# Attention of a two-layer decoder trunk: score products grouped over two PSUM banks, q's inverse RMS applied in the softmax, and a new order of the attention stage on every engine

## The chip, the core and the metric

One core of a Trainium2 chip runs the whole program. The metric is the device time of one execution in microseconds (us). The core has five engines, each with its own instruction stream that it works off in order, and they meet only at semaphores: PE (TensorE, matmuls; its weight loads are listed as PEld), DVE (VectorE), ACT (ScalarE), POOL (GpSimd) and SP (SyncE, which here only issues DMAs). PE writes to PSUM, eight banks of 512 fp32 columns in 128 partitions; DVE and ACT read it.

## The reference

Two layers (DEPTH = 2) over 256 tokens of width 1024. Each layer has a SwiGLU FFN (hidden width 2816), the mixing stage that is changed here, and a second FFN:

```python
x = x + 0.5 * swiglu(rmsnorm(x, ffn1_norm[l]), ...)
h = rmsnorm(x, mix_norm[l])
c_q, c_kv, k_pe, q_s, k_s, v_s = jnp.split(h @ w_in[l], split_idx, axis=-1)
q_a  = (rmsnorm(c_q, ...) @ mla_w_q_b[l])    # 4 heads, 128 plain + 64 rotary columns
kv_a = (rmsnorm(c_kv, ...) @ mla_w_kv_b[l])  # 4 heads, 128 of k + 128 of v
q_a, k_a = rmsnorm(q_a, mla_q_norm[l]), rmsnorm(k_a, mla_k_norm[l])   # per head, then rotary on the 64
out_a = dense_causal_attention(q_a, k_a, v_a, mla_scale)
q_b, k_b = apply_rope(rmsnorm(q_s, ...)), apply_rope(rmsnorm(k_s, ...)) # 8 q heads, 2 k heads, 64 columns
out_b = sliding_window_sink_attention(q_b, k_b, v_b, swa_sinks[l], swa_scale)   # window 128, sinks
x = x + concat(rmsnorm(out_a, ...), rmsnorm(out_b, ...)) @ w_o[l]
x = x + 0.5 * swiglu(rmsnorm(x, ffn2_norm[l]), ...)
```

All products are of fp32 accuracy.

## The kernel before

The order on every engine is written out by hand; there is no scheduler. The 256 tokens are two blocks, t = 0 and t = 1, of 128 rows. The weights come as a stream of halves of 128 x 1024 fp32 through a ring of four raw buffers (SP issues, one DMA for each half). ACT rounds a half to fp32r (`whi`, L444) and DVE subtracts to get the rest (`wlo`, L747); these two are called a split. A large product is three fp32r matmuls, hi x hi, hi x lo, lo x hi (L1125, L1128, L1129; a `product`). The six weight slots are freed by PE as it goes on.

The mixing stage of a layer runs as follows. `input_main` and `input_tail` give the input projection of both blocks in banks A[t] and UV[t]. For each block, ACT and DVE take squares, POOL raises the sums to the power -0.5, DVE normalises (`latent_norm`), PE transposes (`transpose_latent`), and `latent_products` gives the latent heads' q, k and v. Then all of q and k is brought to its final form before it is transposed: `mla_parts` and `mla_sums` (squares of q and k together), one POOL step for both, `mla_norm` and `window_norm` (multiplication by the inverse RMS, the gains, the rotation), `transpose_qk` (17 transposes for each block) and copies to `qt` and `kt`. The scores of a block fill banks A[t][0] and A[t][1] in turn: two latent heads in a bank, then window heads, four in a bank for block 0 and two for block 1. For each head `scores` issues a 128-row fp32 product (L1347), a 64-row one for the rotary part (L1349) and a bf16 product of the identity with the mask (L1351); a window head has a 64-row product (L1355) and a mask (L1357). An fp32 product is listed as two MATMUL instructions (two passes), an fp32r or bf16 one as one. After a bank come `maxima` (DVE), `softmax` (ACT, exponentials with their sums, L644), `transpose_probs` (PE, L1368), `probs_copy` (ACT, L658) and `values` (PE, L1385). Block 0's output is normalised, transposed (`transpose_norm`) and multiplied by `w_o` in eight `output_chunk`s, of which five are put between the banks of block 1; then come block 1's eight, and the second FFN.

Of the kernel before, what the change touches and what calls it, by code (L numbers as in the profile page):

```python
# [17 lines left out]
ALU = mybir.AluOpType  # L18
# [6 lines left out]
P = 128  # L25
D = 1024
# [87 lines left out]
def hybrid_trunk(nc, x_in, stream, norm_gains, norm_cols, small_gains, col_gains, rope, out):  # L114
    with ExitStack() as ctx:
# [23 lines left out]
        rot_in, rot_tmp = rot[:, 0:640], rot[:, 640:1280]  # L139
        attn = sb("attn", [P, D])  # L140
        kpe_g = attn[:, D - ROPE:D]
        kpe = heads(attn[:, 512:512 + TB * ROPE], TB)
        xg = xn
# [9 lines left out]
        probs = work[:, 0:2, :]  # L153
# [12 lines left out]
        consts = sb("consts", [P, 3, 10])  # L166
# [8 lines left out]
        ss_m = sb("ss_m", [P, TB, 8])  # L175
# [28 lines left out]
        rstd_ready = sem("rstd_ready")  # L204
        xn_ready = sem("xn_ready")
# [23 lines left out]
        sum_ready = sem("sum_ready")  # L229
        main_done = sem("main_done")  # L230
# [7 lines left out]
        swa_copied = sem("swa_copied")  # L238
        swa_ss = sem("swa_ss")
        swa_rstd = sem("swa_rstd")  # L240
        swa_used = sem("swa_used")
        mla_done = sem("mla_done")
        mla_squares = sem("mla_squares")
        mla_ss = sem("mla_ss")
        mla_rstd = sem("mla_rstd")
        qkn_ready = sem("qkn_ready")
        qk_psum = sem("qk_psum")
        qk_act = sem("qk_act")
        qk_dve = sem("qk_dve")
# [10 lines left out]
        def norm_no(l, k, t):  # L260

            return (l * NORMS + k) * TB + t

# [53 lines left out]
        def score_banks(t):  # L317
            per = 4 // (t + 1)
            return [(True, [0, 2]), (True, [1, 3])] + [(False, list(range(i, i + per))) for i in range(0, SH, per)]
# [29 lines left out]
        def _(pool):  # L349
# [5 lines left out]
            pool.memset(consts[:, 1, :], EPS)  # L355
            pool.memset(consts[:, 0, :], -0.5)
# [26 lines left out]
            def norm_rstd(l, k, t):  # L383
                n, rs = 2 * norm_no(l, k, t), rs_x[:, t, 0:1]
                if k == 2:
                    pool.wait_ge(ss_ready, n + 2)
                    rstd(rs_x[:, t, :], ss_x[:, t, :], consts[:, 1, 0:2], rstd_ready)
                    return
# [7 lines left out]
                step(pool.tensor_tensor(eps_x[:, t, :], rs.to_broadcast([P, 10]), consts[:, 1, :], ALU.mult))  # L396
# [3 lines left out]
            def latent(l, t):  # L400
                pool.wait_ge(latent_ss, l * TB + (t + 1))
                rstd(rs_c[:, t, :], ss_c[:, t, :], eps_x[:, t, 0:2], latent_rstd)
# [5 lines left out]
            def mla(l, t):  # L408
                pool.wait_ge(mla_ss, l * TB + (t + 1))
                rstd(rs_m[:, t, :], ss_m[:, t, :], consts[:, 1, 0:8], mla_rstd)  # L410

            for l in range(DEPTH):
                norm_rstd(l, 0, 0)
                if l == 0:
                    pool.dma_start(cs[:], rope.rearrange("t p a d -> p t a d")).then_inc(rope_loaded, 16)
                    load_gain(0, 3)
# [4 lines left out]
                load_gain(l, 2)  # L421
# [1113 lines left out]
```

## Time and profile before

| | |
|---|---|
| time, median of 3 runs | 965.27 us (965.18 to 965.64) |
| the profiled execution: its time, its span | 965.41 us, 963.6 us |
| PE busy, PEld busy | 943.1 us, 792.4 us |
| DVE, ACT, POOL busy | 638.8, 527.3, 58.9 us |
| granted TensorE clock | 1.000 of full speed |
| HBM | 171 GB/s over the span |

The span is from the first to the last instruction of the profiled execution. A busy time is the union of the engine's instructions; those of PE overlap at their ends, so what an instruction costs PE is read from one start to the next. The mixing stage of layer 0 lies at about 198 to 300 us, that of layer 1 at about 673 to 776 us.

### The profile page before, as it was taken

To read this page: it belongs to the slowest core of one execution; us is meant where nothing else is said; L and a number is where in the kernel's file an instruction comes from. 1 tells how busy PE (TensorE), PEld (TensorE's weight loads), DVE (VectorE), ACT (ScalarE), POOL (GpSimd) and SP (SyncE) were. 2 spreads that over 40 slices of the span, in tenths; PEclk is the share of its full clock that TensorE was granted. 3 is DMA by queue.
4 is the path that set the end of the run, shared out by engine and by line. 5 is a ranking of instruction groups with operands and counts; after the bars stand their busy time and mean duration, and the time that the engine had idled before them with its cause. 6 is when DMAs were issued, how large, how long until landed. Compare 5 with 4: busy or idle time off the path is not lost. (4 is left out here: it accounts for less than half of the span.)

```text
span 963.6 us, 14627 instructions
## 1 busy us (share of the span) xinstructions
PE 943.1 (98%) x4998; PEld 792.4 (82%) x4998; DVE 638.8 (66%) x941; ACT 527.3 (55%) x1018; POOL 58.9 (6%) x100
## 2 busy tenths in 40 slices
PE   7999999999899999999999999999998999999998
PEld 5888888888677888888878888888876788888887
DVE  5766666677766766666666666667777666666663
ACT  7555555564665655555555555556456655555551
POOL 3000000032111000000010000000330100000000
PEclk9999999999999999999999999999999999999999
DMA  8755555550054765555547555555401547555541
GB/s 303 263 190 186 191 195 184 187 197 2 22 167 151 252 194 192 183 191 195 175 155 236 191 195 183 190 195 175 153 1 49 170 155 235 185 188 196 185 163 44
DMA packets 45812, 165.41 MB, mean 172 GB/s; under 512 B 5296, under 2 KB 5296, under 8 KB 45776
## 3 DMA queue, kind: packets, MB, share of 16 engines
q1 hardware_dynamic: 44496, 160.98, 50.6%
q0 software_dynamic: 992, 3.42, 1.0%
q8 instruction: 23, 0.38, 0.2%
q10 hardware_dynamic: 288, 0.54, 0.1%
q14 instruction: 13, 0.11, 0.0%
HBM read 163.86 MB, written 1.05 MB: 171 GB/s over the span
## 5 line engine op out<-in xcount | busy, mean ns | idle before, releaser
L747 DVE TENSOR_TENSOR wlo<-raw,whi 128x1024 fp32r<-128x1024 f32 x304 | 370.6, 1224 | 130.7 <-ACT whi L444 130.4
L444 ACT ACTIVATE whi<-raw 128x1024 fp32r<-128x1024 f32 x304 | 316.8, 1051 | 10.3 <-DMA raw<-stream 10.3
L1186 PE MATMUL UV<-acts,whi 128*128 128x512 f32 x1280 | 318.9, 391 | 0.0
L1186 PEld LDWEIGHTS UV<-acts,whi 128*128 128x128 f32 x1280 | 234.9, 188 | 46.9 <-DVE wlo L747 1.5
L1193 PEld LDWEIGHTS UV<-acts,wlo 128*128 128x128 f32 x1280 | 174.3, 190 | 12.2
L1193 PE MATMUL UV<-acts,wlo 128*128 128x256 f32 x1280 | 178.8, 282 | 0.0
L1125 PE MATMUL A<-whi,ht_hi 128*128 128x512 f32 x352 | 138.2, 393 | 0.0
L1128 PE MATMUL A<-wlo,ht_hi 128*128 128x512 f32 x352 | 137.9, 392 | 0.0
L1129 PE MATMUL A<-whi,ht_lo 128*128 128x512 f32 x352 | 137.0, 389 | 0.0
L507 ACT ACTIVATE ht_hi<-work 128x256 fp32r<-128x256 f32 x80 | 33.4, 418 | 121.9 <-DVE work L826 121.9
L503 ACT ACTIVATE work<-UV 128x256 f32<-128x256 f32 x80 | 30.7, 383 | 88.7 <-PE UV L1193 88.6
L495 ACT ACTIVATE work<-UV 128x256 f32<-128x256 f32 x80 | 30.6, 383 | 87.0 <-PE UV L1193 87.0
L1129 PEld LDWEIGHTS A<-whi,ht_lo 128*128 128x128 f32 x352 | 66.1, 188 | 14.4
L1125 PEld LDWEIGHTS A<-whi,ht_hi 128*128 128x128 f32 x352 | 66.4, 189 | 11.6
L1128 PEld LDWEIGHTS A<-wlo,ht_hi 128*128 128x128 f32 x352 | 66.4, 189 | 10.7
L821 DVE TENSOR_TENSOR work<-UV,work 128x256 f32<-128x256 f32 x80 | 33.9, 424 | 50.7 <-ACT work L503 50.7
L831 DVE TENSOR_TENSOR ht_lo<-work,ht_hi 128x256 fp32r<-128x256 f32 x80 | 34.0, 425 | 38.7 <-ACT ht_hi L507 38.7
L1125 PE MATMUL A<-whi,acts 128*128 128x512 f32 x136 | 54.9, 403 | 0.0
L1129 PE MATMUL A<-whi,acts 128*128 128x512 f32 x136 | 53.2, 391 | 0.0
L1128 PE MATMUL A<-wlo,acts 128*128 128x512 f32 x136 | 53.0, 390 | 0.0
L817 DVE TENSOR_TENSOR work<-UV,work 128x256 f32<-128x256 f32 x80 | 33.9, 424 | 24.4 <-ACT work L495 24.4
L390 POOL TENSOR_TENSOR sums<-sums,consts 128x1 f32<-128x1 f32 x12 | 9.7, 805 | 585.2 <-ACT qkn L462 369.7
(166 smaller groups left out, 871.2 us busy)
## 6 DMA issues: line engine op xcount, KB each, us to landing
raw<-stream SPq DMA_DIRECT2D x304, 512.0 KB, 3.4
gain<-norm_gains POOLq DMA_DIRECT2D x5, 512.0 KB, 4.8
out<-x SPq DMA_DIRECT2D x4, 256.0 KB, 2.1
sgain<-small_gains POOLq DMA_DIRECT2D x2, 324.0 KB, 4.8
x<-x_in SPq DMA_DIRECT2D x1, 512.0 KB, 3.5
x<-x_in ACTq DMA_DIRECT2D x1, 512.0 KB, 7.6
cs<-rope POOLq DMA_DIRECT2D x1, 128.0 KB, 5.5
cgain<-col_gains POOLq DMA_DIRECT2D x2, 1.0 KB, 5.4
```

The lines of the kernel that those rows point to most:

```text
L444: act.activation(whi_half(unit, half), raw[:, n % RAW, :], ACT.Copy).then_inc(hi_done, 1)
L503: act.activation(up_b, UV[c][:, 1, SEQ:512], ACT.Copy).then_inc(up_copied, 1)
L507: act.activation(wide_h(g, c)[0], heads(h_w, TB), ACT.Copy).then_inc(h_w_hi_done, 1)
L747: dve.tensor_tensor(wlo_half(unit, half), raw[:, n % RAW, :], whi_half(unit, half).bitcast(F32), ALU.subtract).then_inc(split_done, 1)
L817: dve.tensor_tensor(gate_s, UV[c][:, 0, 0:SEQ], gate_b, ALU.add).then_inc(gate_summed, 1)
L821: dve.tensor_tensor(up_s, UV[c][:, 1, 0:SEQ], up_b, ALU.add).then_inc(up_summed, 1)
L831: dve.tensor_tensor(lo, heads(h_w, TB), hi.bitcast(F32), ALU.subtract).then_inc(h_w_split, 1)
L1125: first = pe.matmul(dst, hi, w_hi, start=start, stop=False, skip_group_check=True)
L1128: pe.matmul(dst, hi, w_lo, start=False, stop=False, skip_group_check=True)
L1129: return pe.matmul(dst, lo, w_hi, start=False, stop=stop, skip_group_check=True)
L1186: last = pe.matmul(UV[c][:, j, :], whi_half(unit, j)[:, k * P:(k + 1) * P], acts[:, :, k, :], start=k == 0, stop=False, skip_group_check=True)
L1193: last = pe.matmul(UV[c][:, j, 0:SEQ], wlo_half(unit, j)[:, k * P:(k + 1) * P], act_hi[:, :, k, :], start=False, stop=k == KD - 1, skip_gr ...
```

## The change

- Scores. `latent_scores` issues the four 128-row products of a block first, then the four 64-row rotary products, by turns from rows 0 to 63 into bank 0 and from rows 64 to 127 into bank 1, and then one mask product for each bank over both heads. `window_masks` writes the masks of two banks first (512 columns each); `window_scores` adds the 64-row products of these two banks, again by turns of row half and bank. Block 1 has three groups of two banks: latent heads in A[1], window heads in UV[0], window heads in A[1]; the probabilities of some of them lie in a half of `gain`, so `gain` for the last norm is loaded later.
- The inverse RMS of q is no longer multiplied into q. The scores are those of q without it; `maxima` multiplies the maxima by it and `softmax` takes it as the scale of the exponential (a value for each partition). q is rotated before the sums of its squares are known, and for the window heads the gains are multiplied into the rotation tables by POOL (`rope_tables`).
- k and q of the latent heads have separate squares, POOL steps, waits and copies.
- The order is new on PE, ACT, DVE and POOL. `input_main` of block 1 is done by banks, bank 0 first; bank 1, the tail and the scores of block 0 are interleaved; five chunks of the output projection lie between the banks of block 1 as before, and the last norm and splits stand in another order.

On PE, layer 0, block 0, two of the latent heads of before (names: `qt` and `kt` are q and k transposed, A0 is block 0's pair of banks):

```order
L1347 MATMUL A0<-kt,qt 128x128
L1349 MATMUL A0<-kt,qt 128x128
L1351 MATMUL A0<-masks,ident_b 128x128
L1347 MATMUL A0<-kt,qt 128x128
L1349 MATMUL A0<-kt,qt 128x128
L1351 MATMUL A0<-masks,ident_b 128x128
```

and the same place up to the window heads in the changed kernel, with the rows of the `product`s between them left out:

```order
L1538 MATMUL A0<-kt,qt 128x128 [waits rope_kept,k_nope_kept,q_nope_kept]
L1538 MATMUL A0<-kt,qt 128x128 x3
L1546 MATMUL A0<-kt,qt 128x128 x4
L1551 MATMUL A0<-masks,ident_b 128x256 x2
...
L1589 MATMUL UV0<-ident,work 128x128 [waits swa_k_kept,k_nope_kept,probs_ready]
L1589 MATMUL UV0<-ident,work 128x128
L1562 MATMUL A0<-masks,ident_b 128x512 [waits probs_ready]
L1562 MATMUL A0<-masks,ident_b 128x512
L1589 MATMUL UV0<-ident,work 128x128 [waits pt_ready,probs_ready]
L1589 MATMUL UV0<-ident,work 128x128
L1575 MATMUL A0<-kt,qt 128x128 [waits swa_k_kept,swa_q_kept]
L1575 MATMUL A0<-kt,qt 128x128 x7
```

Products of one kind now follow each other, and a mask product serves two or four heads.

On PE, layer 0, block 1, the latent heads and the first group of window heads in the changed kernel (gain here holds probabilities, A1 and UV0 are score banks), with block 0's norm transposes left out:

```order
L1538 MATMUL A1<-kt,qt 128x256 [waits k_nope_kept,rope_kept,q_nope_kept]
L1538 MATMUL A1<-kt,qt 128x256 x3
L1546 MATMUL A1<-kt,qt 128x256 x4
L1551 MATMUL A1<-masks,ident_b 128x2x128 x2
L1528 MATMUL UV1<-ident,qkn 128x128 [waits k_nope_kept,swa_k_ready]
...
L1562 MATMUL UV0<-masks,ident_b 128x512 [waits attn_ready]
L1562 MATMUL UV0<-masks,ident_b 128x512
L1575 MATMUL UV0<-kt,qt 128x256 [waits swa_k_kept,swa_q_kept]
L1575 MATMUL UV0<-kt,qt 128x256 x3
L1589 MATMUL UV1<-ident,gain 128x128 [waits swa_k_kept,k_nope_kept,probs_ready]
```

Before, this block's banks had one score bank ahead of each transposition of probabilities; now two banks are written together.

On ACT, layer 0, block 0, the squares of before (qkn is where squares are thrown away, `ss_part` their sums):

```order
L614 ACTIVATE qkn,ss_part<-UV0 128x128 [waits mla_done]
L614 ACTIVATE qkn,ss_part<-UV0 128x128 x3
L614 ACTIVATE qkn,ss_part<-A0 128x128 x4
L687 ACT_TABLE_LOAD
L687 ACTIVATE sink_gap<-consts 128x1
```

and the same work in the changed kernel, where k's squares, the copy of q and q's squares stand apart:

```order
L715 ACTIVATE work,ss_part<-A0 128x128 [waits kv_done]
L715 ACTIVATE work,ss_part<-A0 128x128 x3
L721 ACTIVATE qkn<-UV0 128x512 [waits q_nope_done]
L726 ACTIVATE UV0,ss_part<-UV0 128x128 [waits q_nope_copied]
L726 ACTIVATE UV0,ss_part<-UV0 128x128 x3
L731 ACTIVATE UV0,ss_part<-UV0 128x64 [waits q_rope_read]
L731 ACTIVATE UV0,ss_part<-UV0 128x64 x3
```

The copy of q (L721) has moved ahead of its squares, and four short squares of q's rotary part have come over from DVE.

The core of the diff:

```diff
@@ scores
-            def scores(l, t, b):
...
-                for j, hd in enumerate(hs):
...
-                        pe.matmul(dst, qt[:, t, hd, :], kt[:, 2 + hd, 0:t + 1, :], start=True, stop=False,
-                        pe.matmul(dst, qt[r:r + ROPE, t, 4 + hd // 2, :], kt[r:r + ROPE, hd // 2, 0:t + 1, :],
-                        last = pe.matmul(dst[:, t * P:wide], ident_b[:], masks[:, 1, :], start=False, stop=True,
+            def latent_scores(l, t):
+                wide = (t + 1) * P
+                pe.wait_ge(q_nope_kept, l * TB + (t + 1))
+                pe.wait_ge(k_nope_kept, l * TB + (t + 1))
+                pe.wait_ge(rope_kept, l * TB + (t + 1))
+                for b in range(2):
+                    for j, hd in enumerate(BANKS[t][b][1]):
+                        nope = pe.matmul(A[t][:, b, j * wide:(j + 1) * wide], qt[:, t, hd, :],
+                                         kt[:, 2 + hd, 0:t + 1, :], start=j == 0, stop=False, skip_group_check=True)
...
+                for j in range(2):
+                    for b in range(2):
+                        hd = BANKS[t][b][1][j]
+                        r = ROPE * (hd % 2)
+                        pe.matmul(A[t][:, b, j * wide:(j + 1) * wide], qt[r:r + ROPE, t, 4 + hd // 2, :],
+                                  kt[r:r + ROPE, hd // 2, 0:t + 1, :], start=False, stop=False,
+                for b in range(2):
+                    dst = heads(A[t][:, b, 0:2 * wide], 2)[:, :, t * P:wide]
+                    pe.matmul(dst, ident_b[:], over_heads(masks[:, 1, :], 2), start=False, stop=True,
+            def window_scores(l, t, b):
+                for j in range(per):
+                    for i in range(2):
+                        hd = BANKS[t][b + i][1][j]
+                        r = SD * i
+                        last = pe.matmul(score_bank(t, b + i)[:, j * wide:(j + 1) * wide],
+                                         qt[r:r + SD, t, 6 + hd % 4, :], kt[r:r + SD, 6, 0:t + 1, :], start=False,
@@ softmax
-                                          scale=MLA_SCALE if latent_heads else SWA_SCALE,
+                                          bias=shift[:, b % 2, j:j + 1], scale=query_rstd(t, b)[:, j:j + 1],
@@ GpSimd's stream
-                    load_gain(0, 3)
...
+                    if k == 2:
+                        pool.wait_ge(pt_psum, bank_no(l, 1, 5) + 1)
+                        load_gain(l, 3)
@@ PE's order after block 0's input projection
-                input_main(l, 1, range(0, 2))
+                input_main(l, 1, range(0, 4), [0])
                 transpose_latent(l, 0)
...
+                input_main(l, 1, range(4, KD), [0])
+                kv_products(l, 0)
+                q_nope_products(l, 0)
+                q_rope_products(l, 0)
+                input_main(l, 1, range(0, 4), [1])
+                transpose_q_nope(l, 0)
+                transpose_k_nope(l, 0)
+                transpose_rope(l, 0)
+                transpose_swa_q(l, 0)
+                input_main(l, 1, range(4, 6), [1])
+                transpose_swa_k(l, 0)
+                latent_scores(l, 0)
+                input_main(l, 1, range(6, KD), [1])
                 transpose_latent(l, 1)
+                input_tail(l, 1, range(0, 4))
                 transpose_probs(l, 0, 0)
+                window_masks(l, 0, 2)
+                transpose_probs(l, 0, 1)
+                window_scores(l, 0, 2)
+                input_tail(l, 1, range(4, KD))
                 values(l, 0, 0)
                 values(l, 0, 1)
+                kv_products(l, 1)
                 transpose_probs(l, 0, 2)
+                q_rope_products(l, 1)
+                q_nope_products(l, 1)
+                transpose_q_nope(l, 1)
+                transpose_probs(l, 0, 3)
@@ ACT's order, block 1
+                kv_squares(l, 1)
+                softmax(l, 0, 3)
+                q_nope_copy(l, 1)
```

## Rows read from the trace of the kernel before

**Rows 1.** The page: busy time of each engine, share of the span, instructions.

```profile
PE 943.1 (98%) x4998; PEld 792.4 (82%) x4998; DVE 638.8 (66%) x941; ACT 527.3 (55%) x1018; POOL 58.9 (6%) x100
```

**Rows 2.** Windows: stretch, length, busy of PE, PEld, DVE, ACT, POOL, clock, DMA share, GB/s.

```profile
229.84:254.31 24.47, 20.82 (x137) 16.50 (x136) 18.86 (x47) 14.81 (x62) 4.41 (x5) 1.00 0.00 1
...
265.44:286.60 21.16, 20.42 (x121) 16.16 (x120) 13.49 (x26) 13.10 (x33) 2.08 (x3) 1.00 0.48 157
```

**Rows 3.** PE by time (start us, us): block 0's four latent heads.

```profile
232.79 0.47 PE L1347 MATMUL A<-kt,qt 128*128 128x128 f32 x2 [0.40 <-ACT kt L634]
233.19 0.48 PE L1349 MATMUL A<-kt,qt 64*128 64x128 f32 x2
...
236.21 0.47 PE L1125 MATMUL A<-whi,acts 128*128 128x512 f32 x1
```

**Rows 4.** PE by time: four window heads of block 0 and what follows them.

```profile
240.06 0.49 PE L1355 MATMUL A<-kt,qt 64*128 64x128 f32 x2
...
242.27 0.66 PE L1385 MATMUL UV<-v_mla,work 128*128 128x128 f32 x4
```

**Rows 5.** PE by time: block 1's four latent heads and what follows.

```profile
254.31 0.67 PE L1347 MATMUL A<-kt,qt 128*128 128x256 f32 x2
254.91 0.70 PE L1349 MATMUL A<-kt,qt 64*128 64x256 f32 x2
...
259.43 0.61 PE L1368 MATMUL UV<-ident,work 128*128 128x128 f32 x4
```

**Rows 6.** PE by time: window heads of block 1, two banks of four.

```profile
259.97 0.70 PE L1355 MATMUL A<-kt,qt 64*128 64x256 f32 x2
260.60 0.28 PE L1357 MATMUL A<-masks,ident_b 128*128 128x256 bf16 x1
260.81 0.70 PE L1355 MATMUL A<-kt,qt 64*128 64x256 f32 x2
...
261.56 1.11 PE L1138 MATMUL UV<-ident,xn 128*128 128x128 f32 x8
...
268.33 0.70 PE L1355 MATMUL A<-kt,qt 64*128 64x256 f32 x2
...
269.84 0.48 PE L1125 MATMUL A<-whi,acts 128*128 128x512 f32 x1
```

**Rows 7.** PE by time: a run of four fp32 products and what follows.

```profile
262.51 1.06 PE L1385 MATMUL UV<-v_mla,work 128*128 128x128 f32 x8
263.40 0.60 PE L1368 MATMUL UV<-ident,work 128*128 128x128 f32 x4
```

**Rows 8.** PE by time: instructions with PE's idle time before them in brackets.

```profile
247.09 1.10 PE L1385 MATMUL UV<-v_swa,work 128*128 128x64 f32 x8 [0.69 <-ACT work L658]
249.34 0.66 PE L1335 MATMUL A<-ident,qkn 128*128 128x128 f32 x4 [1.15 <-DVE qkn L979]
...
252.72 0.76 PE L1335 MATMUL A<-ident,qkn 128*128 128x128 f32 x5 [1.41 <-DVE qkn L918]
...
285.52 1.32 PE L1138 MATMUL UV<-ident,xn 128*128 128x128 f32 x8 [0.73 <-DVE xn L773]
```

**Rows 9.** ACT by time: block 1's squares; a softmax of four heads.

```profile
240.44 0.27 ACT L614 ACTIVATE qkn<-UV 128x128 f32<-128x128 f32 x1
...
243.19 0.38 ACT L658 ACTIVATE work<-UV 128x256 f32<-128x256 f32 x1
...
248.13 0.37 ACT L644 ACTIVATE work<-A,shift 128x128 f32<-128x128 f32 x1 [1.10 <-DVE shift L1010]
...
249.52 0.21 ACT L650 ACTIVATE sink_e<-sink_gap 128x4 f32<-128x4 f32 x1
```

**Rows 10.** The page: DVE's part of a split (busy us, mean ns).

```profile
L747 DVE TENSOR_TENSOR wlo<-raw,whi 128x1024 fp32r<-128x1024 f32 x304 | 370.6, 1224 | 130.7 <-ACT whi L444 130.4
```

**Rows 11.** Windows at the start of the program, columns as in rows 2.

```profile
10.00:15.00 5.00, 3.83 (x14) 2.58 (x15) 5.00 (x12) 4.54 (x12) 0.65 (x1) 1.00 1.01 384
```

**Rows 12.** Waits from 7 to 45 us: us in total, times, longest.

```profile
ACT whi L444 <- DMA raw<-stream: 4.4, 6, 1.1
```

More of the change, by code:

```diff
@@ L421, in _ @@
                 load_gain(l, 2)
+                rope_tables(l)
                 norm_rstd(l, 1, 0)
                 norm_rstd(l, 1, 1)
[L424 to L427 removed]
+                latent(l, 0)
+                window(l, 0)
+                latent(l, 1)
+                latent_keys(l, 0)
+                latent_queries(l, 0)
+                window(l, 1)
+                latent_keys(l, 1)
+                latent_queries(l, 1)
                 for k in (2, 3):
@@ L756, in add_to_x, with norm_apply @@
                                              ALU.mult, ALU.add).then_inc(x_ready, 1)
-            def norm_apply(l, k, t):
+            def norm_apply(l, k, t, banks=range(2)):
                 n = norm_no(l, k, t)
@@ L1079, in _ @@
+                query_rope(l, 1)
+                latent_keys(l, 1)
+                window_keys(l, 1)
+                split(mix + 6, 0)
+                keep_rope(l, 1)
                 window_result(l, 0)
+                norm_apply(l, 2, 0, [0])
+                norm_apply(l, 2, 0, [1])
                 maxima(l, 1, 0)
-                split(mix + 6, 0)
                 maxima(l, 1, 1)
-                norm_apply(l, 2, 0)
                 maxima(l, 1, 2)
                 norm_lo(l, 2, 0)
+                maxima(l, 1, 3)
@@ L1262, in ffn, with input_main @@
                     transpose_norm(l + 1, 0, 0)
-            def input_main(l, t, chunks):
+            def input_main(l, t, chunks, banks=range(2)):
                 for k in chunks:
@@ L1270, in input_main @@
                         half_split(u, hf)
-                    freed = k == 0 if t == 0 else k % 2 == 0 and k > 0
-                    for n in range(2):
+                    freed = k == 0 if t == 0 else k % 2 == 0 and k > 0 and 1 in banks
+                    for n in banks:
                         w = slice(n * 512, (n + 1) * 512)
@@ L1456, in _ @@
-                for k in range(4, KD - 1):
+                transpose_swa_q(l, 1)
+                latent_scores(l, 1)
+                transpose_swa_k(l, 1)
+                transpose_norm(l, 2, 0)
+                window_masks(l, 1, 2)
+                window_scores(l, 1, 2)
+                transpose_probs(l, 1, 0)
+                window_masks(l, 1, 4)
+                window_scores(l, 1, 4)
+                transpose_probs(l, 1, 1)
+                values(l, 1, 0)
+                output_chunk(l, 0, 0)
```

644 lines of the change are left out of this document (390 added, 254 removed).

## The prediction, made before the changed kernel was run

> **What bounds the kernel now.** I read the page first: PE is busy 943.1 of 963.6 us and no other engine comes near it [rows 1]. So the time is PE's own work plus what PE waits, and an edit is worth what it takes from one of the two. The windows come next. The change touches the stage from 198 to 300 us and its twin in layer 1. PE is busy only 20.82 of 24.47 us there from 229.84 to 254.31, and DVE and ACT are busy 18.86 and 14.81 [rows 2]: PE waits for chains that pass through them. The timeline names the waits: 0.40 us ahead of block 0's scores [rows 3], then 0.69, 1.15, 1.41 and 0.73 us [rows 8], 4.4 us in a layer. The reader should also see in the timeline that a busy PE is not an efficient one here: the scores take far longer than their columns, which is the first term below.
>
> **The scores.** What they cost now, start to start: block 0's four latent heads from 232.79 to 236.21, 3.42 us [rows 3]; four of its window heads 240.06 to 242.27, 2.21 us, so eight 4.42 [rows 4]; block 1's latent heads 254.31 to 259.43, 5.12 us [rows 5]; its window heads 1.59 and 1.51 us a bank of two, so four banks 6.2 [rows 6]. Together 19.2 us a layer.
>
> What the pieces cost: four fp32 products of 128 columns in a run (eight instructions) go from 262.51 to 263.40, 0.22 us each [rows 7], but the first one among the scores takes 0.40 [rows 3]. With 256 columns it takes 0.60 [rows 5]; twice 0.22 is 0.44. So each change of the kind of product, between 128 rows, 64 rows and mask, costs some 0.16 to 0.18 us, and before there are two or three to every head. A mask of 256 columns with the change behind it takes 0.21 [rows 6], of which I put 0.1 on the change; 512 columns of mask then take 0.22.
>
> After, with nothing overlapped: block 0's latent heads 4 x 0.22 + 4 x 0.22 + 0.22 for two masks + 0.4 for changes = 2.4; its window heads 0.45 masks + 8 x 0.22 + 0.3 = 2.5; block 1's latent heads 4 x 0.44 + 4 x 0.44 + 0.22 + 0.4 = 4.1; its window heads, twice 0.45 + 4 x 0.44 + 0.3, 5.0. Sum 14.0, a gain of 5.2 us a layer. That is the lower bound.
>
> The products by turns use different halves of the array's rows and different banks. No row here has two such products next to each other, so the trace doesn't show what that is worth: from nothing to half of their time, less one pass at the end of a run. Half would take 0.44 - 0.11 = 0.33 from block 0's latent heads, 0.77 from its window heads, 0.66 and 2 x 0.66 from block 1's, 3.1 us a layer, gain 8.3. I take the half. My ground is that the 64-row products are listed with the tile 64*128 [rows 3], so half of the array is unused in them, and neither operands nor bank are shared with the neighbour; weight loads already run under products. The Trainium skill, TensorEngine Tiling (Array Packing), Key Properties, says that different tiles can execute weight loads and matmuls in parallel; no row before shows it. By that rule the upper gain holds, without it the lower.
>
> **Changes between fp32 and fp32r.** The first fp32r product after the scores has 0.47 us in the record and starts its neighbour some 0.1 later than in a run [rows 3]. I count five more such returns in block 1's input stage than before, none more in the output stage: +0.5 us a layer.
>
> **The waits.** The three waits of 0.69, 1.15 and 1.41 us come while block 1's input is already used up [rows 8]. Now 12 `product`s of it, half of the tail and block 0's probabilities lie between, and q and k are rotated before their sums are known. I followed the new streams by durations of the trace. Up to block 0's softmax nothing is late: k is ready for its transposition just when PE comes to it. After that I find two waits.
> 1. `transpose_q_nope` of block 1 waits for the copy of q, which stands on ACT behind k's squares, v's copy and a softmax. Before, eight squares and the copy of v took 240.44 to 243.19, 2.75 us, so four squares and a copy take about 1.6; the softmax of four heads 248.13 to 249.73, 1.6; the copy 0.5 [rows 9]. That is 3.7 us behind `kv_products`, in which PE has four transposes (0.45) and the 12 products of q (2.1). Say 1.0 us.
> 2. `latent_scores` of block 1 waits for `keep_rope` on DVE, which stands behind a split of 1.22 us [rows 10]; PE comes some 0.5 us early.
> The wait of 0.73 us before block 0's eighth chunk [rows 8] goes, because half of block 1's norm is transposed earlier and the rest behind that chunk.
> A walk like this misses waits; each bank has a chain PE, DVE, ACT, PE, ACT, PE. I add 1.2 us a layer for them: 2.7 us of waits against 4.4, a gain of 1.7.
>
> **What costs nothing.** The table load moves ahead of `swa_copies`; PE has 12 products (2.7 us) and three transposes to do there. The scale of the exponential becomes a value for each partition; even some 0.1 us more on each of a bank's exponentials is hidden in block 1 by an output chunk, and enters wait 1 in block 0. POOL's tables are made during the first FFN, where it is idle. `gain` for the last norm is loaded after the last probabilities are transposed: its 512 KB have until block 1's third chunk, about 8 us; DMA is at 0.48 there [rows 2]. If it came late, `norm_apply`, and every split queued behind it on DVE, would stand with it.
>
> **The start.** One 512 KB load is gone from the first 10 us. DMA is full there (share 1.01, 384 GB/s) [rows 11], so 1.4 us of its time, and ACT waits 4.4 us for raw halves [rows 12]. PE is on that chain only in part: 0.7 us, between 0 and 1.4.
>
> **Sum.** Per layer -8.3 + 0.5 - 1.7 = -9.5, two layers -19.0, start -0.7: 965.4 - 19.7 = 945.7 us, from the profiled execution's own 965.41, which is 0.1 above the median; the difference is below what I can predict. A measurement of this kernel can tell about 0.2% (1.9 us) from no change.
>
> **Rivals.**
> A. The halves don't overlap (the change doesn't do what it says). Gain -5.2 + 0.5 - 1.7 = -6.4 a layer, 965.4 - 12.8 - 0.7 = 951.9; with none of the waits gained 955.3. For it: no row shows an overlap, and an fp32 product is two passes in order. Against it: the half-empty array. Chance 0.2.
> B. DVE and ACT become the bound of the stage. From 229.84 to 254.31 DVE has 18.86 us of work [rows 2]; take 4 us of scores from PE's 20.8 and DVE is ahead of it, unless it loses work too. It does: the products of q with its inverse RMS and with gains are gone, and the rest of its work there can't be less than some 15 us. If half of the gain of the scores turns into waits (4 us a layer) the time is 945.7 + 8 = 954; if all, 962. The Trainium skill, the same page, PSUM Bottleneck, warns of this: tiling speeds up TensorE, not the evacuation of PSUM. Chance 0.1, against it that the new order gives each engine other work between the links.
> C. The other side: PE's clock. All windows have the granted clock at 1.00, the 2.4 GHz level [rows 2], with idle times up to 1.41 us [rows 8]. If a wait of several us (a late gain, or wait 1 longer) let it fall to 1.2 GHz, every us of PE's work until it rises costs one more. It decides from 9.9 us of work at the low level in each layer; with 12 us the time is about 970. Against it: no wait that I find is longer than those of before. The Trainium skill, TensorE: Matmul & The Clock Gate, says that the half rate is the default and activity lifts it; the trace shows it lifted throughout. Chance 0.05.
> D. The waits nearly vanish, as the walk without my addition has it, or fully: -8.3 + 0.5 - 4.4 = -12.2 a layer and 1.4 at the start, 939.6. This belongs to my forecast's own range.
>
> **Numbers.** Forecast with its range 939.6 to 950: 0.63. A (950 to 955.5): 0.2. B (954 to 963): 0.1, C 0.05, and 0.02 for no change by a mix of small things. Reaching from 939.6 to 956 leaves out C, the rest and the worse half of B. Faster: 0.63 + 0.2 + 0.1 less a little of B within 0.2% = 0.92; same 0.03; slower 0.05.
>
> **What would show it.** The start-to-start time of the 64-row products by turns: 0.22 us for two of 128 columns if they overlap, 0.44 if not; the four 128-row products 0.22 or 0.44 each. The score rows in all 10.9 us a layer, or 14. PE's idle time in each mixing stage about 2.7 us, most of it before `transpose_q_nope` and `latent_scores` of block 1. DVE busy less. The output chunks without idle time between them. At the start, shorter waits of ACT for raw halves. I am wrong if PE idles over 5 us in a stage, if the clock has a window under 1.00, or if the products by turns follow each other as in a run of the same half.

## The result and the profile after

| | before | after | difference |
|---|---|---|---|
| median, us | 965.45 | 938.85 | -26.6 |
| range of the runs, us | 965.18 to 965.67 | 938.49 to 939.04 | |
| profiled execution's span, us | 963.6 | 937.0 | -26.6 |

Four runs each; after takes 0.9707 of before, 95% interval 0.9668 to 0.9746. The forecast was 945.7 us, with a range from 939.6 to 956.0: the kernel gained 26.6 us where 19.7 were forecast, and ended 0.75 us below the range. In the series of the experiments the kernel before ran 53 times more: 12 of these executions took 972.6 to 975.5 us, at a mean granted clock of 0.986 to 0.991, and the other 41 took 964.7 to 968.4 us at 0.994 to 0.998.

The page of the changed kernel, to be read against [rows 1]:

```profile
PE 921.4 (98%) x4970; PEld 783.2 (84%) x4970; DVE 627.1 (67%) x953; ACT 535.3 (57%) x1054; POOL 67.4 (7%) x139
```

PE's busy time fell by 21.7 us with only 28 instructions fewer; the rest of the gain is idle time. DVE lost 11.7 us and ACT has 8 us more. In the windows (columns as in [rows 2]) the first two are cut at the first score of block 1, which starts at 247.01 us where it started at 254.31 [rows 5]; the last is the stretch of time of the first row in [rows 2].

```profile
228.00:247.01 19.01, 16.90 (x132) 14.14 (x132) 14.27 (x45) 15.82 (x67) 5.30 (x8) 1.00 0.01 2
247.01:275.00 27.99, 27.55 (x178) 22.51 (x176) 22.85 (x47) 22.39 (x55) 4.41 (x11) 1.00 0.45 149
229.84:254.31 24.47, 21.92 (x160) 17.18 (x159) 18.44 (x54) 21.80 (x84) 6.98 (x12) 1.00 0.06 22
```

In the last one PE is busy 21.92 us and ACT 21.80 of 24.47, where they were busy 20.82 and 14.81 before. The waiting that is left stands ahead of block 1's scores, 2.11 us; behind them PE idles 0.44 us in 28. The clock is at 1.00 throughout this execution, and its mean is 1.000 in all four.

The scores by time on PE (start us, us, line), to be read against [rows 3 to 6]. The columns are the same.

```profile
226.85 1.06 PE L1538 MATMUL A<-kt,qt 128*128 128x128 f32 x8
227.84 0.71 PE L1546 MATMUL A<-kt,qt 64*128 64x128 f32 x8
228.49 0.39 PE L1551 MATMUL A<-masks,ident_b 128*128 128x256 bf16 x2
...
232.41 0.60 PE L1562 MATMUL A<-masks,ident_b 128*128 128x512 bf16 x2 [0.27 <-ACT work L762]
232.85 0.38 PE L1589 MATMUL UV<-ident,work 128*128 128x128 f32 x2
233.16 1.16 PE L1575 MATMUL A<-kt,qt 64*128 64x128 f32 x16
...
242.71 0.65 PE L1497 MATMUL A<-ident,qkn 128*128 128x128 f32 x4 [1.31 <-ACT qkn L721]
...
247.01 1.94 PE L1538 MATMUL A<-kt,qt 128*128 128x256 f32 x8
248.87 1.14 PE L1546 MATMUL A<-kt,qt 64*128 64x256 f32 x8
249.94 0.39 PE L1551 MATMUL A<-masks,ident_b 128*128 128x256 bf16 x2
...
251.25 0.59 PE L1562 MATMUL UV<-masks,ident_b 128*128 128x512 bf16 x2
251.77 1.14 PE L1575 MATMUL UV<-kt,qt 64*128 64x256 f32 x8
252.84 0.66 PE L1589 MATMUL UV<-ident,gain 128*128 128x128 f32 x4
253.93 0.60 PE L1562 MATMUL A<-masks,ident_b 128*128 128x512 bf16 x2 [0.43 <-ACT gain L762]
254.46 1.14 PE L1575 MATMUL A<-kt,qt 64*128 64x256 f32 x8
255.53 0.66 PE L1589 MATMUL UV<-ident,gain 128*128 128x128 f32 x4
```

A row's start to the next row's start is what it costs. Eight 128-row instructions of 256 columns, four products, take 1.86 us (247.01 to 248.87); the eight 64-row ones by turns behind them take 1.07, and the same again in each group of window heads (251.77 to 252.84, 254.46 to 255.53). Sixteen 64-row instructions of 128 columns take 1.09 (they end when an `input_tail` product starts at 234.25). All scores of a layer take 9.66 us, where before they took 19.17.

The waits that PE has left, over both layers (us in total, times, longest):

```profile
PE A L1497 <- ACT qkn L721: 2.6, 2, 1.3
...
PE UV L1589 <- ACT sink_e L767: 1.0, 2, 0.5
PE A L1562 <- ACT gain L762: 0.9, 2, 0.4
...
PE A L1562 <- ACT work L762: 0.5, 2, 0.3
```

**Where the time came from.** By the starts of the same instructions, the start of the program gave 0.85 us (the mixing stage begins at 208.93 instead of 209.78) and each mixing stage 12.9 (90.76 us to 77.88); 0.85 + 2 x 12.9 = 26.6. Within a stage, in layer 0: scores -9.5, PE's waits -2.5, transposes of probabilities, of norms and of the latent part and the values together -1.4, products +0.5. The waits are taken here with the slower first instruction behind each; by recorded idle time alone they are -2.1, and the transposes and values -1.8. The 0.85 us of the start is less sure than the rest (experiment 8).

### The profile page after: what moved, and what is told of

The parts are those of the page before. It is cut to its first block, busy times and chain, and to the rows that moved or that the text cites. A ratio compares the mean times of both kernels' runs of the same rounds, so it can differ in the third digit from the quotient of the medians.

```text
span 937.0 us, 14776 instructions
## 1 busy us (share of the span) xinstructions
PE 921.4 (98%) x4970; PEld 783.2 (84%) x4970; DVE 627.1 (67%) x953; ACT 535.3 (57%) x1054; POOL 67.4 (7%) x139
## 4 chain that ended last, share of the span: by engine, by line
PE 92%; ACT 3%; DVE 2%; issue 1%; DMA 1%; POOL 0%; DVEq 0%; SPq 0%; POOLq 0%
PE UV L1347 31%; PE UV L1354 16%; PE A L1284 11%; PE A L1287 11%; PE A L1288 11%; PE UV L1284 2%; PE UV L1288 2%; PE UV L1287 2%; PE UV L1608 1%; ACT work L762 1%; PE UV L1299 1%; PE UV L1589 1%; DMA raw<-stream 1%; DVE wlo L879 0%; PE A L1575 0%
```

## The experiments

Times are medians. Each kernel ran beside the kernel before, whose medians in the three series were 965.55, 965.49 and 965.69 us. "By stage" means the time in a profiled execution from the first transposition of the latent part to the first product of the FFN after it: 98.05 us before, 85.16 after, in layer 0 (98.02 and 85.19 in layer 1). The line of the first transposition is L1458 in the changed kernel and L1296 in the kernel before. The changed kernel itself was not run again in these series, so a difference to its 938.85 us is one between series; the medians of the kernel before differ by up to 0.24 us.

**1. The same half after the same half.** In the groups, the two products of one bank come ahead of the two of the other (four and four in block 0's window heads).

```
-                for j in range(2):
-                    for b in range(2):
+                for b in range(2):
+                    for j in range(2):
...
-                for j in range(per):
-                    for i in range(2):
+                for i in range(2):
+                    for j in range(per):
```

> The changed kernel, but the 64-row products follow each other by row half (all of bank 0, then all of bank 1) instead of by turns. Theory: by turns, the second pass of one product runs beside the first pass of the next, so a group of n products costs n+1 passes instead of 2n; 3+7 passes of 0.107 us in block 0 and 3+3+3 of 0.213 us in block 1 come back, 3.0 us a layer, less some 0.3 that waits take up: 944.3 us (943.3 to 945.2). Rival: what was gained in the scores came from grouping alone, and turns are worth nothing: 938.9, within 1 us.

Measured: 940.12 us, 1.3 more than the changed kernel. That looked like the rival, which allowed 1 us. The rows of this kernel say why it isn't one:

```profile
233.14 1.71 PE L1575 MATMUL A<-kt,qt 64*128 64x128 f32 x16
234.78 0.36 PE L1284 MATMUL UV<-whi,acts 128*128 128x192 f32 x1
...
249.42 1.14 PE L1546 MATMUL A<-kt,qt 64*128 64x256 f32 x8
250.49 0.39 PE L1551 MATMUL A<-masks,ident_b 128*128 128x256 bf16 x2
```

Eight instructions ordered 2 + 2 products take 1.07 us, just as by turns; sixteen ordered 4 + 4 products take 1.64 instead of 1.09. The edit had not taken the overlap away, only some of it in one place. The expectation had assumed that only neighbours overlap.

**2. The halves kept apart.** So the next one puts a mask, a 128-row product, between the two halves of each group.

```
                for b in range(2):
                    for j in range(2):
                        ...
                        pe.matmul(A[t][:, b, j * wide:(j + 1) * wide], qt[r:r + ROPE, t, 4 + hd // 2, :],
                                  kt[r:r + ROPE, hd // 2, 0:t + 1, :], start=False, stop=False,
                                  skip_group_check=True)
                    ...
                    pe.matmul(dst, ident_b[:], over_heads(masks[:, 1, :], 2), start=False, stop=True,
                              skip_group_check=True).then_inc(scores_done, 1)
```

> The changed kernel, but in each pair of banks the 64-row products of one bank come first, then a mask (a 128-row product), then those of the other bank; no product of one half of the rows stands next to one of the other half. The grouping by kind stays. Theory (the overlap of the halves is about half of the gain in the scores): block 1's three groups of 8 rows go from 1.07 to about 2.1 us, block 0's from 0.65 to 1.0 and from 1.09 to 2.1, with some 0.1 us for each further change of kind: about +5 us a layer, 948.5 to 950 us, if the clock stays at its upper level. Rival (rows of the two halves save nothing beyond the grouping, as the small step of the earlier run with the same half after the same half might suggest): 939 to 941 us.

Measured: 948.78 us, 9.9 more than the changed kernel, as the theory had it. By stage 90.00, 4.84 more.

```profile
251.28 1.13 PE L1546 MATMUL A<-kt,qt 64*128 64x256 f32 x4
252.34 0.28 PE L1550 MATMUL A<-masks,ident_b 128*128 128x256 bf16 x1
252.55 1.13 PE L1546 MATMUL A<-kt,qt 64*128 64x256 f32 x4
253.61 0.28 PE L1550 MATMUL A<-masks,ident_b 128*128 128x256 bf16 x1
```

Four instructions of one half take 1.06 us, as long as eight of both halves together (1.07). This is the overlap: the time is halved. In block 0 four of 128 columns take 0.64 and eight 1.09, so one is 0.11 us and a run of a new kind has 0.19 ahead of it. With these, the overlap alone is worth 8 x 0.22 + 0.18 - 1.07 = 0.87 in each of three groups, 0.91 in block 0's window heads and 0.44 in its rotary products, 4.0 us a layer; five more changes of kind at 0.18 make the other 0.9 of the 4.84.

In every run the half of the rows and the bank change together, so no run takes one without the other. A change of bank alone doesn't seem to do it: the eight 128-row instructions of 256 columns, two products for one bank and then two for the other, take 1.86 us in the changed kernel, no less than 8 x 0.22 = 1.76 for eight that don't overlap, where eight 64-row ones in the same order of banks take 1.07 (experiment 1).

**3. Head by head in the new order.** The order of the change, but each head's products and mask follow each other as before the change.

```
+                        nope = pe.matmul(dst, qt[:, t, hd, :], kt[:, 2 + hd, 0:t + 1, :], start=True, stop=False,
+                                         skip_group_check=True)
...
+                        pe.matmul(dst, qt[r:r + ROPE, t, 4 + hd // 2, :], kt[r:r + ROPE, hd // 2, 0:t + 1, :],
+                                  start=False, stop=False, skip_group_check=True)
+                        last = pe.matmul(dst[:, t * P:wide], ident_b[:], masks[:, 1, :], start=False, stop=True,
+                                         skip_group_check=True)
```

> The changed kernel in its new order, but each head's products and mask issued one after the other as before. Theory: PE is the bound and the scores' 9.5 us a layer count nearly in full, less some 1 us a layer that the waits of the new order take up: 956 us (954 to 958.5). Rival: the order is what gained, and the scores lie beside chains of DVE and ACT that are as long: under 950 us.

Measured: 963.58 us (961.88 to 968.85), 24.7 more than the changed kernel: nearly all of the gain is gone. By the rows, the scores are 2 x 9.5 = 19 us of it, as experiment 6 confirms. The rest is in the windows (stretch, length, busy of PE, PEld, DVE, ACT, POOL, clock, DMA share, GB/s); the execution profiled here is the longest, 968.85 us:

```profile
236.00:238.00 2.00, 1.44 (x10) 0.90 (x9) 1.93 (x5) 2.00 (x7) 0.00 (x0) 1.00 0.00 0
238.00:240.00 2.00, 2.00 (x10) 1.30 (x9) 0.43 (x1) 0.57 (x2) 0.00 (x0) 0.83 0.00 0
240.00:242.00 2.00, 2.00 (x8) 1.27 (x7) 1.27 (x5) 0.00 (x0) 0.00 (x0) 0.50 0.00 0
...
246.00:248.00 2.00, 2.00 (x12) 2.00 (x11) 0.20 (x2) 1.44 (x7) 1.64 (x2) 0.50 0.03 8
248.00:250.00 2.00, 2.00 (x8) 1.62 (x7) 1.46 (x7) 1.28 (x7) 0.52 (x1) 0.61 0.00 0
```

The clock went to half, the 1.2 GHz level, in the middle of block 0's window heads. No wait stands shortly ahead of it but one of 0.56 us; from there on PE is recorded as busy in full. What it did before was a run of small products of changing kinds. A second fall, at 256 us, comes after 1.7 us of idle time between 252 and 256. Two windows of 5 us show it again in layer 1 (0.72 and 0.60 from 715 to 725), and two at the start of the program (0.56 and 0.76 from 10 to 20 us): in this execution the mixing stage begins at 211.79 us instead of 208.93.

**4. Grouping in the old order.** The kernel before, with the products of each bank grouped by kind; no two halves share a group.

```
+                    for j, hd in enumerate(hs):
+                        nope = pe.matmul(bank[:, j * wide:(j + 1) * wide], qt[:, t, hd, :], kt[:, 2 + hd, 0:t + 1, :],
...
+                    for j, hd in enumerate(hs):
+                        r = ROPE * (hd % 2)
...
+                    last = pe.matmul(heads(bank[:, 0:2 * wide], 2)[:, :, t * P:wide], ident_b[:],
```

> The kernel before in its old order, with the products of one bank grouped (128-row products, 64-row products, one mask for the bank), no two banks by turns. Theory: about 6 us of PE's work a layer go, but of block 0's part most turns into longer waits for q and k of block 1, since DVE's chain ends those: 3.7 us a layer stay, 958 us (955.5 to 960.5). Rival: PE's work counts in full in the old order too: 953.4 us.

Measured: 959.59 us (958.71 to 959.94), 6.0 less than before and inside the range of the theory, though not for its reason alone. By stage 94.66 in layer 0, 3.4 less, and 95.53 in layer 1, 2.5 less. Here too the clock falls, which it doesn't in the profiled execution of the kernel before:

```profile
245.00:250.00 5.00, 3.75 (x21) 3.62 (x22) 4.62 (x13) 3.36 (x12) 0.97 (x1) 0.70 0.01 3
250.00:255.00 5.00, 5.00 (x29) 3.81 (x28) 2.68 (x7) 3.27 (x9) 0.27 (x2) 0.96 0.00 0
...
715.00:720.00 5.00, 3.01 (x19) 2.42 (x18) 4.62 (x15) 2.99 (x16) 1.84 (x2) 0.80 0.00 0
720.00:725.00 5.00, 5.00 (x26) 4.88 (x25) 2.98 (x7) 3.45 (x7) 0.00 (x0) 0.51 0.00 0
```

The mean clock is 0.992 to 0.996 in all ten executions, where 41 of the 53 executions of the kernel before have 0.994 to 0.998 and the other 12 less than 0.992. So this run gives no clean price for the grouping: part of the gain was given back at the low clock.

**5. Full products beside the heads.** The kernel of 3, plus six mask products of 512 columns, which nothing reads, ahead of block 0's window heads.

```
+                for _ in range(6):
+                    pe.matmul(A[0][:, 0, :], ident_b[:], over_heads(masks[:, 1, :], 4), start=True, stop=True,
+                              skip_group_check=True)
```

> The earlier run in the new order with the heads scored one by one (963.6 us, clock at the 1.2 GHz level from 239.6 to 249.4 us and from 256 to 259.7), plus six mask products of 512 columns, which nothing reads, ahead of block 0's window scores, in each layer: 1.3 to 1.6 us of added work in each. Theory (the clock falls there because the stretch of small products leaves TensorE little to do, and its loss is part of that run's 24.7 us): the granted clock stays at 1.00 or is low for a shorter time, and the kernel is faster than that run in spite of more work, 957 to 961 us. Rival (the clock's fall costs nothing, since the stage waits for other engines anyway, or full products do not hold it): 966 to 967 us.

Measured: 965.01 us (962.76 to 969.0), between the two expectations. The trace has one layer of each kind. In layer 0 the clock stays at 1.00, and the stage takes 95.97 us in spite of 1.3 us of added work, where the kernel of 3 took 100.20. In layer 1 the clock falls (0.79 and 0.52 in the windows from 710 to 720, 0.66 from 725 to 730) and the stage takes 100.14; the kernel of 3 took 97.33 there, with a low clock too. One group of full products is not enough to hold it each time.

**6. More of them.** Three such groups: ahead of block 0's first score, ahead of its window heads, and between the two banks of these.

```
+                    if i and t == 0:
+                        for _ in range(6):
+                            pe.matmul(A[0][:, 1, :], ident_b[:], over_heads(masks[:, 1, :], 4), start=True,
+                                      stop=True, skip_group_check=True)
```

> The new order with the heads scored one by one, and three groups of six mask products of 512 columns that nothing reads in each layer: ahead of block 0's first score, ahead of its window scores, and between the two banks of these. 18 x 0.22 = 4.0 us of added work a layer. Theory (the small products let the clock fall, and full ones beside them hold it): the clock is at 1.00 in both layers; the grouping is then worth 9.5 us a layer, 938.9 + 19 + 8 = 965.9 us, 965 to 967, and repeated runs lie closer together than the 7 us of the run without fillers. Rival (fillers do not hold it): low windows in both layers and 968 to 972 us.

Measured: 966.40 us, inside the range of the theory, and the clock is at 1.00 in the whole profiled execution. Nine of the ten executions took 965.55 to 967.08 us; the tenth took 3322.73 us, and nothing on record says why. The mean clock is 0.998 or 1.000 in all ten, where it was 0.989 to 0.996 in experiment 5 on the same chip. For instance:

```profile
240.00:245.00 5.00, 5.00 (x31) 3.30 (x31) 2.09 (x7) 0.00 (x0) 0.00 (x0) 1.00 0.00 0
...
715.00:720.00 5.00, 5.00 (x29) 3.12 (x29) 1.56 (x6) 0.00 (x0) 0.00 (x0) 1.00 0.00 0
```

Less the 8 us of added work that is 958.4: the change with its scores head by head at the full clock, 19.5 above 938.85, where the rows give 2 x 9.5. What the low clock costs the kernel of 3 is 963.6 - 958.4, some 5 us by the medians. Its profiled execution is its longest: by stage it took 100.20 and 97.33 us, where this one took 98.55 in both layers, 94.6 without the added work, so 5.6 and 2.7 us. The pair shows it without the durations too: more work of full products, waits of much the same length (at most 1.3 us before q's transposes, 1.7 in the kernel of 3), and no fall.

**7. Constants in the exponential.** The scale of each exponential and of the maxima is a constant; q's inverse RMS is left out of the result.

```
-                                          bias=shift[:, b % 2, j:j + 1], scale=query_rstd(t, b)[:, j:j + 1],
+                                          bias=shift[:, b % 2, j:j + 1], scale=MLA_QK ** -1.0 if latent_heads else SD ** -1.0,
```

> The changed kernel with a constant as the scale of the exponential, and of the maxima, in place of q's inverse RMS (the inverse RMS of q is left out of the result; its making stays). Theory: the value for each partition costs each exponential 0.095 us, 24 a layer, and the part of it ahead of PE's waits (8 exponentials before the copy of q of block 1, 4 before the second masks of block 1) comes back: 1.2 us a layer, 936.5 us. Rival: it is hidden: 938.9 us.

Measured: 937.56 us, 1.3 less, between the two expectations. By stage 84.36, 0.80 less, and as much in layer 1. On ACT, two neighbouring exponentials of the changed kernel and then two of this one:

```profile
240.23 0.44 ACT L762 ACTIVATE work<-A,shift,rs_s 128x128 f32<-128x128 f32 x1
...
240.66 0.45 ACT L762 ACTIVATE work<-A,shift,rs_s 128x128 f32<-128x128 f32 x1
...
240.37 0.35 ACT L762 ACTIVATE work<-A,shift 128x128 f32<-128x128 f32 x1
...
240.71 0.36 ACT L762 ACTIVATE work<-A,shift 128x128 f32<-128x128 f32 x1
```

An exponential of 128 columns starts 0.345 us after its neighbour instead of 0.44, one of 256 columns 0.45 instead of 0.545 (means over several): 0.095 more for a scale that is read per partition. The wait ahead of q's transposes has 1.0 instead of 1.3 us, and the waits at L1589 and L1562 are gone:

```profile
PE A L1497 <- ACT qkn L721: 2.0, 2, 1.0
```

The Trainium skill, ScalarE: Activation LUTs, What ACT_TABLE_LOAD costs, gives about 93 ns for each operand of an activation that is read per partition; the trace agrees.

**8. The gain's load back at the start.** A 512 KB load in the first microseconds, from which nothing is computed.

```
+                    pool.dma_start(gain[:, 1, :], norm_gains[3:4, :].to_broadcast([P, D])).then_inc(early_gain, 16)
```

> The changed kernel with the 512 KB load of a gain back in the first microseconds, as before the change; nothing is computed from it. Theory (the start gained 0.85 us because that load shared the full DMA queues with x and the first weights): 939.6 to 939.8 us. Rival (the start's 0.85 us came from something else): 938.8 to 939.0 us.

Measured: 939.63 us, 0.8 more than the changed kernel. The mixing stage is as long as without it (85.18 by stage), so the 0.8 us lie outside it. That fits the theory, but it is not shown firmly. The stage begins at 210.36 us in this trace, the longest execution of its six, and the traces of experiments 1, 2, 5, 6, 7, 9 and 10, which leave the start as it is in the changed kernel, have it anywhere from 208.90 to 209.83. The start differs by 0.9 us for no change at all, as much as it is said to have gained. What speaks for the load is that the six executions here (939.08 to 940.26) all lie above the changed kernel's four (938.49 to 939.04).

**9. q copied by VectorE.** Block 1's q goes from its bank to SBUF on DVE; ACT loses that work, `keep_rope` comes ahead of the split, and PE makes q's 128-row products ahead of its rotary ones (not shown).

```
-                q_nope_copy(l, 1)
...
+                query_copy(l, 1)
                 query_rope(l, 1)
...
-                split(mix + 6, 0)
                 keep_rope(l, 1)
+                split(mix + 6, 0)
```

> The changed kernel, but block 1's copy of q out of its bank is made by VectorE instead of ScalarE, q's 128-row products come before its rotary ones, and VectorE copies the transposed rotary parts before it splits a weight half. Theory (ScalarE is without a gap from 235.9 to 247.1 us, so the wait of 1.31 us before the transposes of block 1's q is its work; PE comes to block 1's scores when ScalarE has copied k): the scores of block 1 start 0.5 to 0.8 us earlier, 937.3 to 937.9 us. Rival (the wait only moves to the transposes of k or of the rotary parts, which stand behind the same squares): 938.5 to 939.2 us.

Measured: 940.66 us, 1.8 more than the changed kernel and above both expectations. By stage 85.72, 0.56 more, and about as much in layer 1; the other 0.7 us lie outside the stage and are not explained. The wait of 1.3 us became three:

```profile
243.05 0.63 PE L1593 MATMUL UV<-ident,work 128*128 128x128 f32 x4 [0.67 <-ACT work L777]
...
244.96 0.63 PE L1525 MATMUL A<-ident,qkn 128*128 128x128 f32 x4 [0.44 <-DVE qkn L1135]
...
247.15 1.89 PE L1542 MATMUL A<-kt,qt 128*128 128x256 f32 x8
...
251.57 0.66 PE L1303 MATMUL A<-ident,xn 128*128 128x128 f32 x4 [0.59 <-DVE xn L907]
```

The scores start at 247.15 instead of 247.01. Counted from the start of the stage (209.18 here, 208.93 in the changed kernel) that is 0.1 us earlier, where 0.5 to 0.8 was expected. And PE waits 0.59 us for the norm on DVE, behind the split that is now later. The theory fell: ACT's work is not alone in setting the time of the scores; DVE has no room for it either.

**10. q copied first.** The same work on each engine in another order: ACT copies q and a bank of probabilities ahead of a softmax, and PE follows.

```
-                softmax(l, 0, 3)
                 q_nope_copy(l, 1)
                 probs_copy(l, 0, 2)
+                softmax(l, 0, 3)
```

> The changed kernel, but in layer's block 1 ScalarE copies q and block 0's third bank of transposed probabilities before the softmax of the fourth bank, and TensorE's order follows: q's rotary and 128-row products, then the third bank's transposes, q's transposes, the third bank's values, the rotary transposes, the fourth bank's transposes. No engine has more or less work. Theory (the wait of 1.31 us is part of a stretch in which ScalarE has no gap, so only its total counts): the first score of block 1 moves by less than 0.4 us and the wait shows up elsewhere; 938.2 to 939.2 us. Rival (the order on ScalarE alone makes the wait): two waits of 1.3 us go, 936.3 to 937 us.

Measured: 941.46 us (938.97 to 943.06), 2.6 more, outside both expectations. The wait for q's copy shrank to 0.25 us; 0.95 and 0.29 us stand further back instead, together 1.49 where it was 1.31, so the waits only moved, as the theory says. The first score, though, comes 1.6 us later, counted from the start of the stage. What neither had foreseen is the clock:

```profile
245.00:250.00 5.00, 4.71 (x23) 4.25 (x22) 3.12 (x8) 3.41 (x15) 2.47 (x5) 0.50 0.30 105
250.00:255.00 5.00, 5.00 (x29) 3.67 (x27) 2.66 (x6) 3.62 (x7) 0.74 (x2) 0.83 0.00 0
```

Transposes and small products with short waits between them now stand together from 242 us on, and block 1's scores begin at half the clock. In two of the six executions the mean clock is 1.000, and these took 938.97 and 939.54 us; so at the full clock the new order costs 0.5 us or less. No version tried here that computes the whole reference beats the changed kernel.

## Why the prediction was off

**The mechanism was right; the sum failed in its terms.** The gain of 26.6 us is 6.9 more than forecast: transposes and values 2.8, scores 2.4 (overlap 1.8, grouping 0.6), waits 1.6, the start 0.15. The step that failed most is a term that the sum put at nothing and gave no reason for: what the transposes and values would gain, measured at 1.4 us a layer. With it the forecast would have been 942.9. The next is the overlap, 3.1 us a layer forecast and 4.0 measured. The lower end of the range, 939.6 us, is the sum with all waits gone and 1.4 us for the start. Neither happened: 2.5 us a layer of waits are left. That the time lies only 0.75 us below that end is luck: other terms happened to add up to nearly the same. None of the three signs of being wrong that the prediction named came.

**The scores** (forecast -8.3 a layer, measured -9.5). The term that was mis-sized is the overlap: I took "half of their time, less one pass", 3.1 us. The runs show 4.0: eight instructions of both halves take as long as four of one, with nothing left over at the end of a run. The other 5.5 is the grouping, for which I had 5.2 as the lower bound; changes of kind at 0.16 to 0.18 us were right (0.18 and 0.19 in experiment 2), so fewer of them must be left than I counted. By group, forecast and measured: block 0's latent heads 2.07 and 1.78, its window heads 1.73 and 1.53, block 1's latent heads 3.44 and 3.16, its window heads 3.68 and 3.19.

**Rival A**, that the halves don't overlap, priced the kernel at 951.9; the kernel that keeps them apart measured 948.8. The rule of the Trainium skill, TensorEngine Tiling (Array Packing), Key Properties, holds here for fp32 products of 64 rows, and the trace has its number: 1.07 us for both halves, 1.06 for one.

**The waits** (forecast -1.7 a layer, measured -2.5). Wait 1, `transpose_q_nope` of block 1 for q's copy, was foreseen at 1.0 us and has 1.31; 0.3 of it is the scale's price, which experiment 7 takes away. Wait 2, `latent_scores` for `keep_rope`, didn't come: ACT's copy of k and PE's own transposes end later. In place of the 1.2 us added for waits that a walk misses, three came, 0.27, 0.51 and 0.43, together 1.2. The sum of recorded waits, 2.5, is near the 2.7 forecast. What differs is what a wait costs from start to start: 5.7 us a layer before and 3.2 after, where the brackets have 4.6 and 2.5. I had set 4.4 against 2.7, brackets that leave out the slower first instruction behind each wait. The 4.4 also left out the last wait of the stage:

```profile
293.89 1.32 PE L1138 MATMUL UV<-ident,xn 128*128 128x128 f32 x8 [0.22 <-DVE xn L773]
```

**Returns to fp32r** were forecast at +0.5 us and measured at +0.5.

**Not in the sum:** transposes and values, 1.4 us a layer. Four transposes of probabilities took 0.52 to 0.60 us in most places and now mostly take 0.41 to 0.46; eight of the window's values took up to 0.99 and 1.10 and now 0.81 to 0.87: they too stand behind a change of kind less often. This is counted from rows, and its cause is argued, not tested.

**What costs nothing.** The scale costs 0.65 us a layer by the medians (1.3 in the whole kernel) and 0.80 by stage, 0.3 of it in wait 1 as written and the rest mostly in the waits at L1589 and L1562, for which I had nothing. `gain` came late: DVE waited for it, as the prediction feared, and PE didn't notice.

```profile
278.85 1.42 DVE L908 SCALAR_TENSOR_TENSOR xn<-x,sums,gain 128x512 f32<-128x512 f32 x2 [1.20 <-DMA gain<-norm_gains]
```

**The start** was forecast at 0.7 us and measured at 0.85 in one pair of traces. Experiment 8 gives 0.8 of it back, but the start differs as much between kernels that have it alike, so the size is not shown.

**Rival B**, ACT and DVE as the bound, is where the stretch ahead of block 1's scores stands now, not what decided: ACT is busy without a gap from 235.9 to 247.1 us. Experiment 9 shows it from the other side, since moving a part of its work to DVE gains nothing; experiment 10 says less, as its clock fell.

**Rival C**, the clock, is the one that I had too small. It was put down to a wait of several us. In experiments 3, 4, 5 and 10 the clock falls with no wait over 2 us in the stage, in stretches of small products. It falls in the kernel before as well: 12 of its 53 later executions are some 8 us longer at a mean clock of 0.986 to 0.991. No trace was kept of those, so where it falls in them is not known; the prediction had only one trace, at 1.00. The change is not clear of it by much: experiment 10 swaps a few calls and is in it. Had the products been left head by head, the new order alone would have ended at 963.6 us, 0.2% below before.

## What to carry to other kernels

Group small products by kind (rows, type), and let those that fill half of the array's rows stand together with others of the opposite half: the first saves about 0.18 us at each change of kind, the second halves the time, and by turns isn't needed: four instructions of one half and then four of the other did as well, and of eight and eight only a part of the saving was lost. When a stage consists of small products, read the granted clock of its windows after each edit, also where no wait is long; a part that is slower may be so through the clock, and full products added beside it show whether it is. Compare the mean clock of all executions too, not only of the one that is profiled. In both experiments that rearranged full engines the waits only moved: count each engine's work up to the instruction that is waited for before changing its order.

## What had not been expected of the hardware

- The halves of the rows overlap over a distance: 2 + 2 products of one half after the other take 1.07 us, as by turns; of 4 + 4 a part is still saved (1.64 us against 1.09 by turns, and 2.0 estimated with no overlap from 16 x 0.113 + 0.19).
- The clock falls to its 1.2 GHz level while PE is recorded as busy in full, behind waits of 0.56 us (experiment 3) or 0.95 and 0.29 us (experiment 10). In experiment 3 it stays there for some 10 us (239.3 to 249.5). Three groups of full products in between held it in all ten executions (experiment 6); one group did not (experiment 5). The Trainium skill, TensorE: Matmul & The Clock Gate, A second HAM failure mode: psum-queue depth-cycling, tells of a kernel that idles briefly and often between groups of products and whose clock goes up and down; what is seen here is of that kind, and in experiment 3 PE has no idle time on record for the 2 us ahead of the first fall.
